# A two-block network: router weights loaded in the mixers, the first expert pair gathered in the routing stage, and the gathers of the token stage cut in two

## What is computed

```python
x = _layer_norm(ALPHA * x + mix, ln1_g[i], ln1_b[i])
grp_logits = (xf @ w_grp + b_grp)                  # 512 tokens, 4 groups
g_idx = argmax(grp_logits)
exp_logits = (xf @ w_exp + b_exp)                  # 8 experts in each group
top_l, top_e = lax.top_k(in_grp, 2)                # two experts of the chosen group
gate = p_grp[:, None] * jax.nn.softmax(top_l, axis=-1)
hdn = jax.nn.silu(xb @ w_gate[e]) * (xb @ w_up[e]) # w_gate, w_up: 1024 x 512
return hdn @ w_down[e]                             # 512 x 1024
```

## Time and profile before

| what | us |
|---|---|
| runs | 2744.41, 2740.08, 2737.75 (median 2740.08) |
| the profiled execution | 2749.82 |
| its span | 2748.0 |
| first routing stage, begin to end of projection | 1313.2 to 1378.9 |
| first token stage, first pairs | from 1391.5 |
| second routing stage, begin to end of projection | 2164.3 to 2230.1 |
| second token stage | from 2242.7 |

### The profile page before, as it was taken

The page is one execution under the profiler, slowest core; times in us unless marked ns, Lnnn a source line. Parts: engine busy times, 40 slices in busy tenths (PEclk is TensorE's granted clock), DMA queues, the critical chain, the costliest instruction groups (busy, mean ns, idle before and its releaser), DMA issues. The chain is left out here.

```text
span 2748.0 us, 42579 instructions
## 1 busy us (share of the span) xinstructions
PE 2522.1 (92%) x17694; PEld 1273.5 (46%) x17694; DVE 913.8 (33%) x2037; ACT 646.9 (24%) x1329; POOL 259.8 (9%) x249
## 2 busy tenths in 40 slices
PE   7999898999999999999899998998998899999896
PEld 3554785443433334445444444443356544444442
DVE  2656353412211121567453110013525572210004
ACT  4423763310110010333221110112334221111101
POOL 0100363200000000000110000000004120000001
PEclk9999898999999999999999999999999999999999
DMA  9324305789999963001579999996004149999996
GB/s 322 109 74 161 103 7 199 303 365 427 428 429 428 428 276 133 24 0 62 188 303 406 427 428 428 427 417 214 0 1 191 51 184 371 427 426 427 428 427 262
DMA packets 117170, 735.83 MB, mean 268 GB/s; under 512 B 28695, under 2 KB 32051, under 8 KB 77440
## 3 DMA queue, kind: packets, MB, share of 16 engines
q1 hardware_dynamic: 105808, 703.12, 62.7%
q0 software_dynamic: 7488, 29.10, 2.7%
q10 hardware_dynamic: 3696, 1.06, 0.2%
HBM read 708.31 MB, written 32.55 MB: 270 GB/s over the span
## 5 line engine op out<-in xcount | busy, mean ns | idle before, releaser
L2650 PE MATMUL bank<-ring,expert_in 128*64 128x512 f32 (+1 forms) x1840 | 427.9, 593 | 17.8 <-DMA ring<-in_moe_w_up_dram 8.0
L2668 PE MATMUL bank<-ring,hidden_T 128*64 128x512 f32 (+1 forms) x896 | 226.9, 595 | 34.7 <-ACT hidden_T L2524 29.8
L2650 PEld LDWEIGHTS bank<-ring,expert_in 128*64 128x64 f32 (+1 forms) x1840 | 135.9, 128 | 237.4 <-issue 237.2
L2379 DVE TENSOR_TENSOR hidden<-silu_gate,bank 128x512 f32<-128x512 f32 x32 | 33.7, 1054 | 576.3 <-PE bank L2650 462.8
L2620 PE MATMUL bank<-onehot,x_part 128*128 128x128 bf16 x3072 | 178.0, 220 | 0.0
L2620 PEld LDWEIGHTS bank<-onehot,x_part 128*128 128x128 bf16 x3072 | 173.2, 98 | 2.4 <-issue 2.4
L1956 PE MATMUL bank<-ring,expert_in 128*64 128x512 f32 x768 | 169.7, 598 | 4.9 <-DMA ring<-in_w_gate_dram 4.9
L2668 PEld LDWEIGHTS bank<-ring,hidden_T 128*64 128x64 f32 (+1 forms) x896 | 67.1, 129 | 137.2 <-issue 101.8
L2508 ACT ACTIVATE expert_in<-bank 128x512 f32<-128x512 f32 x64 | 35.0, 595 | 400.3 <-PE bank L2620 400.3
L2650 PE MATMUL bank<-home,expert_in 128*64 128x512 f32 (+1 forms) x320 | 112.4, 593 | 8.0 <-DMA ring<-in_moe_w_up_dram 8.0
L3611 PE MATMUL bank<-x_cols,ring 128*128 128x512 f32 x256 | 112.5, 593 | 1.3 <-PEq L220 1.3
(11 more groups left out here) (718 smaller groups left out, 3932.3 us busy)
## 6 DMA issues: line engine op xcount, KB each, us to landing
ring<-in_moe_w_gate_dram SPq DMA_DIRECT2D x48, 2048.0 KB, 22.9
ring<-in_moe_w_down_dram SPq DMA_DIRECT2D x44, 2048.0 KB, 27.5
ring<-in_moe_w_up_dram SPq DMA_DIRECT2D x42, 2048.0 KB, 25.1
ring<-in_w_gate_dram SPq DMA_DIRECT2D x24, 2048.0 KB, 23.3
ring<-in_w_up_dram SPq DMA_DIRECT2D x24, 2048.0 KB, 21.1
ring<-in_w_down_dram SPq DMA_DIRECT2D x24, 2048.0 KB, 26.7
ring<-in_w_mod_dram SPq DMA_DIRECT2D x12, 2048.0 KB, 10.0
home<-in_moe_w_gate_dram SPq DMA_DIRECT2D x8, 2048.0 KB, 16.9
```

Of the source, the lines that this page charges most:

```text
L2650: mm = pe.matmul(B[2 + 2 * part][rows, :], xe[:, c, rows], ws[e](c), start=(c == 0), stop=(c == NC - 1))
L2668: mm = pe.matmul(B[6 + b][rows, :], hT[:, c, rows], ws[e](c)[:, b * COLS:(b + 1) * COLS], start=(c == 0), stop=(c == NF - 1))
```

## The change

- **Router loads.** The six loads of a layer's router weights, biases and norm columns are issued by SP in the mixer that precedes (`load_router`), into memory of their own.
- **First routing stage.** The places of turns, logits and counts between the products, and DVE's order, are written out anew for the first layer. In the second layer the places stay as they were.
- **First pair in the routing stage.** DVE makes the one-hots of pair 0 block by block; PE gathers pair 0 there in place of idle products, with the last block's parts at the end; ACT copies `expert_in`. The differences of the last block's split are taken by DVE (`split_last`), no longer by POOL.
- **Token stage.** It starts with pair 0's gate products. DVE makes pair 1's one-hots first; its product of pair 0 (`hide(0)`) stands between the two sets of tables. Each later gather is cut: first half before the transposes, second half after them (for pair 1: after pair 0's down). ACT copies `hidden_T` before `expert_in`.

Core of the diff:

```diff
+        self.router_w, self.router_b = sb("second_router_w", [P, NC, 36]), sb("second_router_b", [P, 36])
+        self.ln_cols = sb("second_ln_gain_and_shift_cols", [P, 2, NC])
...
+def load_router(m, eng, I, i):
+
+    at = 0
+    for name in ("grp", "exp"):
+        k = I[f"moe_w_{name}_2"].shape[2]
+        eng.dma_start(m.router_w[:, :, at:at + k], I[f"moe_w_{name}_2"][i].rearrange("(c p) e -> p c e", p=P)).then_inc(m.router_here, 16)
+        eng.dma_start(m.router_b[:, at:at + k], I[f"moe_b_{name}_2"][i].partition_broadcast(P)).then_inc(m.router_here, 16)
+        at += k
+    for j, name in enumerate(("g", "b")):
+        eng.dma_start(m.ln_cols[:, j, :], columns(I[f"ln1_{name}_2"][i]), allow_slow_non_contiguous=True).then_inc(m.router_here, 16)
 
 
...
-        oh = sb("onehot", [P, NT, 2, SLOTS], BF16)
-        xe = sb("expert_in", [P, NC, P])
+        oh, xe = R.oh, R.xe
...
-                    wait(dve, onehot_ready, x)
+                    wait(dve, onehot_ready, x - 1)
...
+                    hide(x)
+
+                def hide(x):
                     dve.wait_ge(silu_ready, x + 1)
...
-                onehots(0)
...
+                rows_of_slots(0)
+                onehots(1)
...
+                hide(0)
...
-                pair(0)
...
-                    act.wait_ge(gathered, x + 1)
-                    wait(act, m.weights_used, used(x - 1, 2))
-                    input_half(0)
+                    act.wait_ge(m.weights_used, used(x - 1, 2))
+                    if isinstance(x, int) and x == 1:
+                        act.wait_ge(half_gathered, 1)
+                        input_half(0)
+                        act.wait_ge(gathered, x + 1)
+                    else:
...
+                    act.wait_ge(hidden_turned, x + 1)
+                    act.activation(hT[:, :, :], B[3][:, :].rearrange("p (c s) -> p c s", c=NF), ACT.Copy).then_inc(hidden_T_ready, 1)
                     if not isinstance(x, int) or x < pairs - 1:
                         inputs(x + 1)
-                    act.wait_ge(hidden_turned, x + 1)
-                    act.activation(hT[:, :, :], B[3][:, :].rearrange("p (c s) -> p c s", c=NF), ACT.Copy).then_inc(hidden_T_ready, 1)
...
-                act.wait_ge(half_gathered, 1)
-                input_half(0).then_inc(half_input, 1)
-                act.wait_ge(gathered, 1)
-                input_half(1).then_inc(input_ready, 1)
...
-                def gather(x):
-                    pe.wait_ge(onehot_ready, x + 1)
-                    wait(pe, input_ready, x)
-                    wait(pe, rows_known, x)
+                def begin_gather(x):
+                    pe.wait_ge(onehot_ready, x)
+                    wait(pe, input_ready, x - 1)
+                    pe.wait_ge(rows_known, x)
                     filled_slots()
-                    gather_half(0)
-                    gather_half(1).then_inc(gathered, 1)
+                    mm = gather_half(0)
+                    if x == 1:
+                        mm.then_inc(half_gathered, 1)
...
-                        gather(x + 1)
+                        begin_gather(x + 1)
...
+                    if 0 < x < pairs - 1:
+                        gather_half(1).then_inc(gathered, 1)
...
                     down(x)
-
-                m.idle_products(pe, 7, 2)
-                pe.wait_ge(onehot_ready, 1)
-                gather_half(0).then_inc(half_gathered, 1)
+                    if x == 0:
+                        gather_half(1).then_inc(gathered, 1)
+
                 pe.wait_ge(one_made, 1)
-                filled_slots()
-                gather_half(1).then_inc(gathered, 1)
+                filled_slots().then_inc(gathered, 1)
                 for x in range(pairs):
...
-                at = 0
-                for name, k in (("grp", GR), ("exp", E)):
-                    sp.dma_start(w[:, :, at:at + k], I[f"moe_w_{name}_2"][i].rearrange("(c p) e -> p c e", p=P)).then_inc(router_here, 16)
-                    sp.dma_start(b[:, at:at + k], I[f"moe_b_{name}_2"][i].partition_broadcast(P)).then_inc(router_here, 16)
-                    at += k
-                for j, name in enumerate(("g", "b")):
-                    sp.dma_start(ln_cols[:, j, :], columns(I[f"ln1_{name}_2"][i]), allow_slow_non_contiguous=True).then_inc(router_here, 16)
...
+                both = 1 in begun
+                turns_at = {(1, 0, 7): 0, (2, 0, 4): 1, (3, 0, 5): 2} if both else {(1, 0, 5): 0, (2, 0, 5): 1, (3, 0, 5): 2}
+                logits_at = {(2, 0, 1): 0, (2, 1, 0): 1, (3, 1, 1): 2} if both else {(1, 1, 1): 0, (2, 1, 1): 1, (3, 1, 1): 2}
+                counts_at = {(2, 1, 3): 0, (3, 0, 0): 1, (3, 1, 7): 2} if both else {(1, 1, 7): 0, (2, 1, 7): 1, (3, 1, 7): 2}
...
-                m.idle_products(pe, 0, 1)
...
+                def gather(t, half, parts):
+                    for part in parts:
+                        for c in range(4 * half, 4 * half + 4):
+                            mm = pe.matmul(B[half][:, c % 4 * P:(c % 4 + 1) * P], R.parts[part][:, t, c * P:(c + 1) * P], R.oh[:, t, :, :],
+                                           start=(t == 0 and part == 0 and c % 4 == 0), stop=(t == NT - 1 and part == 2 and c % 4 == 3))
+                    return mm
...
+                pe.wait_ge(evacuated, 2 * (NT - 1))
+                pe.wait_ge(onehot_ready, 2)
+                pe.wait_ge(low, 2 * 2)
+                gather(0, 0, range(3))
                 turn(NT - 1, 1)
-                m.idle_products(pe, 0, 1)
+                gather(0, 1, range(3))
+                gather(1, 0, range(3))
                 logits(NT - 1)
-                m.idle_products(pe, 2, 3)
+                gather(1, 1, range(3))
+                pe.wait_ge(evacuated, 2 * NT)
+                m.idle_products(pe, 3, 2)
                 count(NT - 1)
+                pe.wait_ge(onehot_ready, 3)
+                pe.wait_ge(low, 2 * 3)
+                for half in range(2):
+                    gather(2, half, range(3))
+                pe.wait_ge(onehot_ready, 4)
+                for half in range(2):
+                    pe.wait_ge(high, 2 * 3 + half + 1)
+                    gather(3, half, (0,))
+                for half in range(2):
+                    pe.wait_ge(mid, 2 * 3 + half + 1)
+                    gather(3, half, (1,))
+                for half in range(2):
+                    pe.wait_ge(low, 2 * 3 + half + 1)
+                    gather(3, half, (2,)).then_inc(gathered, 1)
 
             @block.scalar
             def _(act):
@@ -3325,10 +3370,14 @@
                         root(t)
                     upper(t)
                     middle(t)
+                for h in range(2):
...
+                for h in range(2):
+                    act.wait_ge(gathered, h + 1)
+                    act.activation(R.xe[:, 4 * h:4 * h + 4, :], B[h][:, :].rearrange("p (c s) -> p c s", c=4), ACT.Copy).then_inc(input_ready, 1)
+                act.wait_ge(input_ready, 2)
...
-                for t in range(NT):
+                for t in range(NT - 1):
...
+                def onehot(t):
+                    if t == 0:
+                        dve.wait_ge(tables_ready, 3)
+                    dve.wait_ge(pos_ready, 2 * t + 2)
+                    dve.tensor_tensor(R.oh[:, t, :, :], lane, R.pos[:, 0:2, t:t + 1].to_broadcast([P, 2, SLOTS]), ALU.is_equal).then_inc(onehot_ready, 1)
+
+                def split_last():
+                    t = NT - 1
+                    for h in range(2):
+                        dve.wait_ge(high, 2 * t + h + 1)
+                        dve.wait_ge(low, 2 * (t - 1) + h + 1)
+                        dve.tensor_tensor(half(chunked(rest[:, :]), h), half(by_chunk(X[:, t, :]), h), half(chunked(R.parts[0][:, t, :]), h),
+                                          ALU.subtract).then_inc(less, 1)
+                    for h in range(2):
+                        dve.wait_ge(mid, 2 * t + h + 1)
+                        dve.wait_ge(less, 2 * t + h + 1)
+                        dve.tensor_tensor(R.parts[2][:, t, cut(h)], rest[:, cut(h)], R.parts[1][:, t, cut(h)], ALU.subtract).then_inc(low, 1)
+
                 dve.memset(one16[:, :], 1.0).then_inc(tables_ready, 1)
...
+                if 1 in begun:
+                    take(1, 0)
+                    centre_router()
+                    tables()
+                    norm(0)
+                    take(1, 1)
+                    route(0)
+                    norm(1)
+                    take(2, 0)
+                    route(1)
+                    place(0)
+                    onehot(0)
+                    take(2, 1)
+                else:
...
+                onehot(2)
                 place(3)
+                onehot(3)
+                split_last()
...
+                load_router(m, sp, I, 0)
...
+                load_router(m, sp, I, 1)
```

93 lines of the change are left out of this document (50 added, 43 removed).

## The result

Each kernel ran four times: the changed one took 2703.2 to 2714.8 us, median **2710.4**; the one before 2737.8 to 2744.4 us, median 2741.8. The ratio is 0.9871, with a 95% interval of 0.9849 to 0.9892: faster by 1.3%, more than the 0.3% that such a measurement can tell. The forecast was 2707.2 us, in a range of 2698 to 2726. The profiled execution after took 2714.8 us (span 2712.7), 35.0 less than that of before; the forecast was 32.9 less.

A forecast was written before the change was run, and what follows sets the result against it. Expert-weight transfers were taken to bound the token stages late, PE and its waits the routing stages. Stage gains 21.1 + 15.4 = 36.5, less 3.6 for the clock, give 32.9 us: 2740.1 - 32.9 = 2707.2 us, range 2698 to 2726.

The forecast's parts named there:

- What bounds the kernel, and the queue: Token stages: the end is the last load issue into an empty queue, after pair 1's down projection, plus fixed bytes.
- some 4: Token stage start to pair 1's down: transfers fill 52 of 55.7 us, leaving a gap of some 4 us.
- near 380: Token stage: transfer rate in GB/s from stage start to pair 1's down, named as a sign to look for.
- Part 1: Routing stages: router loads moved into the mixers end PE's stall; projections 13.0 and 6.2 us shorter.
- the first one of that part: Routing stages: PE stands still until router weights are in and folded; idle before projection end 11.4 and 5.3 us.
- rival B: First routing stage: new order makes PE wait for DVE, three places at 2.6 us; 2715 us, chance 0.14.
- Issues of SP: Mixers: six router loads hold SP's queue at most 29 us, 40 and 76 us before stage end; cost nothing.
- Part 2: Routing stage: first pair gathered there, its first product at P (projection end) + 14.7; 7.1 and 8.2 us sooner.
- Part 3: Token stage: gather cut in two, hidden_T copied first; 1.0 us sooner after two pairs, later pairs gain nothing.
- Clock: First pair's products: PE partly at 1.2 GHz, costing 1.8 us per stage, bounds 0 and 3.0.
- Rival E: Token stages: longer waits for up weights lower the clock in some 16 pairs; slower, 2760 us, chance 0.04.
- a granted clock under 1.00 between pairs 8 and 15: Token stages: sign that the prediction is wrong, PE's clock being throttled after longer waits for up weights.

The follow-up runs named there:

- split_on_pool: The changed kernel with the last row block split on GpSimd again instead of VectorE; ratio 0.9874 to the kernel before.
- changed_again: The changed kernel run once more, unchanged, beside the other follow-up kernels; ratio 0.9843 to the kernel before.

## Why the prediction was right, and where it was not

- **What bounds the kernel, and the queue: right.** The end follows the last issue into an empty queue, after pair 1's down projection: a delay ahead of it counts in full, 14 us later it costs next to nothing. The idle time left was 7.8 and 8.9 us, where the forecast said "some 4": 49.5 and 49.7 us worth of transfers ran in windows of 57.3 and 58.6 us, for 52 in 55.7. So the rate was 370 and 363 GB/s instead of "near 380". It changed nothing, because a gap stayed.
- **Part 1: right in sum, wrong in its cause, under-sized.** Forecast 13.0 and 6.2 us, measured 15.2 and 7.4 on the projections. The step that failed is the first one of that part, which put the whole of the 11.4 idle us to the router's weights. In the first layer the loads alone give 7.1 us; the wait for chosen_experts grows from 2.6 to 5.2 us in place of the removed one. The other 8.1 us come from the new order, which the forecast had only looked through for new stalls. Its rival B had PE wait for VectorE in this stage, but put that down to the new order, where it did not occur; it came with the old one. The sum came out because the change has both. The size was 2.2 and 1.2 us short: the time that PE lost to the clock was put at 2.0 and 1.5 us, and its busy time fell by 54.27 - 50.46 = 3.8 and 60.54 - 57.54 = 3.0. The small waits that stay are 0.0 and 0.9 us (0.4 and 0.6).
- **Issues of SP: the sum held by luck.** The six loads were bounded by 29 us of queue; they took 28.6 in the odd mixer, 48 us before its end. The bound was six times 4.81 us, called the dearest, but the same load had taken 5.88 us in the first routing stage of before, and one alone took 22.08 here. What held is that nothing stands behind them.
- **Part 2: right, P + 14.7 against P + 14.5.** Most terms too: the route 3.4 us cheaper (3.5), the split 3.5 (3.4), the copy 1.1 (0.9). From the last norm to the last place it is 4.0 us (4.5), and from the copy to the first product 1.1 (0.7); these two misses nearly cancel. The forecast gave 7.1 and 8.2 us; measured 7.3 and 8.4. GpSimd's part in the dear operations, only argued then, is shown by `split_on_pool`.
- **Part 3: right.** Only the first pairs count. At full clock pair 1 ends 55.5 us after the first product instead of 56.4, 0.9 us for the 1.0 forecast.
- **Clock: right in size.** Forecast 1.8 us per stage, bounds 0 and 3.0; measured 1.4 and 2.8, and 0 to 2.9 over the 18 stages that had the gather but no idle products in the pause. That it differs between executions of one kernel was not foreseen.
- **Rival E: half of its mechanism came, and none of its price.** The prediction named a granted clock under 1.00 between pairs 8 and 15 as a sign of being wrong. The sign came: it is 0.98 over the window from 2285, and 64 products take 8.59 us where 7.0 is full clock. It was a poor sign, since the time did not follow. The longest waits of PE for up weights, of the kernel before (first token stage) and of the changed one (second):

```profile
PE bank L2650 <- DMA x_cols<-in_moe_w_up_dram: 5.1, 2, 3.3
```

```profile
PE bank L2669 <- DMA ring<-in_moe_w_up_dram: 15.9, 6, 3.6
```

Before, the granted clock was 1.00 there in spite of a wait of 3.3 us. After, with more of them, it falls in some pairs and not in others. The Trainium skill's rule (TensorE: Matmul & The Clock Gate, "HAM oscillation — how this bites in real kernels") thus agrees with the trace on the clock in part, and on the time not at all: from pair 1 to the end it is 406.1 and 404.1 us, where before had 407.7 and 405.7, because PE waits for the next transfer anyway.
- **The sum.** From the start of the projection to pair 1's down projection the terms give 15.2 + 7.3 + 0.9 - 1.4 = 22.0 us in the first layer and 7.4 + 8.4 + 0.9 - 2.8 = 13.9 in the second, 35.9 together against 32.9 forecast. Part 1 gave 3.4 more than forecast and part 2 0.4; part 3 gave 0.2 less, and the clock took 0.6 more. The fixed stretch behind was 1.6 us shorter in each layer, within its scatter: 39.1. The unchanged rest took 4 us more in that execution. So 35 came out against one execution and 31.4 between the medians; changed_again was 43.9 us below the runs of before beside it. Part of the nearness to the forecast is luck: its terms were 3 us short.

## What to carry to other kernels

Before counting a wait as a gain, ask what the engine would wait for next if it were gone, and from whom the first wait had bought time: in the first projection half of the gain needed a second edit, the order of the work. In a stage bound by transfers only what lies ahead of the last issue into an empty queue counts; behind it a loss is free as long as PE makes it good from its waits for weights, as it did with 14 us and with the lower clock, and a gain is worth nothing. And where runs scatter by 0.3%, read the changed stages by themselves in the profile: the columns up to pair 1 told differences of 1 us, at equal granted clock, that no ratio can, while whole layers still scatter by 2 to 3.

## What the runs showed that I had not expected

One small load held SP's queue for 22 us of the 28.6 that the six took together. The timeline of SP in the odd mixer of the changed kernel, where `load_router` (L244) broadcasts four biases to 128 partitions, and then the same load in the even mixer:

```profile
2069.51 22.08 SPq L244 DMA_DIRECT2D second_router_b<-in_moe_b_grp_dram  x1
...
2093.02 3.10 SPq L244 DMA_DIRECT2D second_router_b<-in_moe_b_exp_dram  x1
```

```profile
1151.20 0.58 SPq L244 DMA_DIRECT2D second_router_b<-in_moe_b_grp_dram  x1
```

In the routing stages before, the same load took 5.88 and 4.81 us. Ahead of it in the odd mixer stand six loads of 2 MB issued in the 8 us before; in the even mixer it is one of 1 MB and one of 16 KB, and nothing else for 39 us. That it waits for the loads ahead fits these four times, but no run here tests it. What it means is that such a load has to stand where nothing queues behind it, and that its cost in one place says little of its cost in another.
